# Small SBUF tiles allocated ahead of the large ones in a one-core, two-layer transformer kernel

## The reference, cut to what matters

```python
h = h + nsa_mixer(rmsnorm(h, mix_norm_g), ...)         # w_in 2048 x 5168, compression, w_out 2048 x 2048
z = rmsnorm(h, ffn_norm_g) @ ffn_w_in                  # 2048 x 11264
h = h + (silu(z[..., :D_FF]) * z[..., D_FF:]) @ ffn_w_out   # 5632 x 2048
x = rmsnorm(h, final_norm_g)
proj = _rmsnorm(x, norm_pre_w) @ w_in_2                # 2048 x 16400
... conv + silu, mLSTM over 4 chunks of 64, group pooling ...
merged = sigmoid(g_a) * (y_a @ w_proj_mlstm) + sigmoid(g_b) * (y_b @ w_proj_pool)
return x + _rmsnorm(merged @ w_out_2, norm_post_w)
```

## Time and profile before

| | |
|---|---|
| time, median of 3 runs | 2233.95 us (2227.65 to 2236.28) |
| the profiled execution | 2227.66 us; its span from first to last instruction 2225.6 us |
| TensorE busy (matmuls) | 2175.0 us, 98% |
| weight loads busy | 1894.7 us, 85% |
| VectorE, ScalarE, GpSimd busy | 1453.6 us, 1030.8 us, 176.8 us |
| mean granted TensorE clock | 0.991 |
| chain of work that ended last | 93% TensorE, 4% VectorE |

### The profile page before, as it was taken

How to read it: one execution, slowest core, us unless ns; L and a number is a source line. 1 busy time by engine, 2 the same in 40 slices (tenths; PEclk the granted TensorE clock), 3 DMA queues, 4 the chain that set the end, 5 groups by cost and what they waited for, 6 DMA issues and landing times.

```text
span 2225.6 us, 35012 instructions
## 1 busy us (share of the span) xinstructions
PE 2175.0 (98%) x12502; PEld 1894.7 (85%) x12502; DVE 1453.6 (65%) x1793; ACT 1030.8 (46%) x1342; POOL 176.8 (8%) x215
## 2 busy tenths in 40 slices
PE   8999999999999999999999999999999999999996
PEld 6887889888888888888888888888888888888885
DVE  7746555676666666656666687766867676566575
ACT  4445555354444444443334455444454454444443
POOL 5000222200000000001222000000000000000022
PEclk8999999999999999999999999999999999999998
DMA  6557433365656565655555455555555555555553
GB/s 233 191 189 239 131 107 116 132 200 179 201 181 198 174 204 181 199 186 174 179 182 173 166 180 176 187 168 177 189 163 179 170 188 179 195 189 186 187 181 103
DMA packets 111562, 395.62 MB, mean 178 GB/s; under 512 B 12178, under 2 KB 16290, under 8 KB 111472
## 3 DMA queue, kind: packets, MB, share of 16 engines
q1 hardware_dynamic: 109344, 386.97, 53.4%
q0 software_dynamic: 2128, 7.38, 1.0%
HBM read 389.83 MB, written 2.13 MB: 176 GB/s over the span
## 4 chain that ended last, share of the span: by engine, by line
PE 93%; DVE 4%; issue 1%; ACT 1%; DMA 1%; POOL 0%; ACTq 0%; DVEq 0%; SPq 0%; POOLq 0%
PE set L1367 51%; PE set L1368 26%; PE set L1379 4%; PE set L1380 2%; DVE w_hl L744 1%; DVE x_hl L774 1%; DMA raw<-in_weights 1%; PE set L1357 1%; PE set L1355 1%; PE set L1356 1%; PE misc L1532 1%; PE set L1342 1%; PE set L1344 1%; PE set L1343 1%; PE misc L1518 1%
## 5 line engine op out<-in xcount | busy, mean ns | idle before, releaser
L744 DVE TENSOR_TENSOR w_hl<-raw,w_hl 128x1024 fp32r<-128x1024 f32 x730 | 911.4, 1258 | 573.9 <-ACT w_hl L491 568.6
L1367 PE MATMUL set<-x_hl,w_hl 128*128 128x512 f32 x3584 | 1265.3, 397 | 10.7 <-DVE x_hl L774 9.6
L491 ACT ACTIVATE w_hl<-raw 128x1024 fp32r<-128x1024 f32 x730 | 764.1, 1056 | 856.7 <-PE set L1368 730.5
L1368 PE MATMUL set<-x_hl,w_hl 128*128 128x256 f32 x3584 | 1005.0, 280 | 0.0
L1367 PEld LDWEIGHTS set<-x_hl,w_hl 128*128 128x128 f32 x3584 | 673.9, 188 | 163.8 <-issue 13.3
L1368 PEld LDWEIGHTS set<-x_hl,w_hl 128*128 128x128 f32 x3584 | 679.3, 190 | 0.8
L1367 PE MATMUL set<-f_hl,w_hl 128*128 128x512 f32 x704 | 249.7, 398 | 4.1 <-DVE w_hl L744 4.1
L1368 PE MATMUL set<-f_hl,w_hl 128*128 128x256 f32 x704 | 198.7, 282 | 0.0
L1367 PEld LDWEIGHTS set<-f_hl,w_hl 128*128 128x128 f32 x704 | 133.0, 189 | 37.3 <-DVE w_hl L744 5.1
L498 ACT ACTIVATE cross<-set 128x512 f32<-128x512 f32 (+1 forms) x152 | 88.5, 582 | 138.4 <-PE set L1368 126.9
L1379 PE MATMUL set<-w_hl,x_hl 128*128 128x512 f32 x384 | 134.3, 394 | 4.7 <-DVE w_hl L744 4.7
(11 more groups left out here) (291 smaller groups left out, 2014.3 us busy)
## 6 DMA issues: line engine op xcount, KB each, us to landing
raw<-in_weights SPq DMA_DIRECT2D x730, 512.0 KB, 4.1
bias_g<-bias POOLq DMA_DIRECT2D x4, 572.0 KB, 3.7
cur<-in_cur POOLq DMA_DIRECT2D x4, 535.0 KB, 3.9
h<-in_x SPq DMA_DIRECT2D x4, 512.0 KB, 7.2
bias<-u_dram POOLq DMA_DIRECT2D x1, 2048.0 KB, 13.6
out<-y_t SPq DMA_DIRECT2D x4, 512.0 KB, 3.3
w<-in_w POOLq DMA_DIRECT2D x1, 256.0 KB, 6.8
vm<-in_causal POOLq DMA_DIRECT2D x1, 192.0 KB, 4.3
```

Source lines behind the costliest of these rows:

```text
L491: a(w_hl[at.slot(j)][:, 0, :], raw[at.slot(j)][:, :], ACT.Copy).then_inc(hi_ready, 1)
L744: tt(w_hl[s][:, 1, :], raw[s][:, :], w_hl[s][:, 0, :].bitcast(F32), ALU.subtract).then_inc(lo_ready, 1)
L1367: mm(o, w[:, 0, c], hl[:, kt, :, :], start=first and k == 0, stop=False, skip_group_check=True)
L1368: last = mm(o[:, S:2 * S], w[:, 1, c], hl[:, kt, 0, :], start=False, stop=True, skip_group_check=True)
```

## The change

The tiles `gains`, `gain2`, `rms`, `rtmp`, `ident` and `ones`, and an unused new tile `lead` of 80 bytes, are allocated before `raw` rather than behind `h` and `cross`. In the attention scope `s1c`, `prob` and `bias_g` are allocated before `o_hl`. Nothing else differs: the instructions of every engine, their order and their semaphores are the same, two lines of the file further down.

```diff
+    gains = sb("gains", [P, 5, KT])
+    gain2 = sb("gain2", [P, KT])
+    rms = sb("rms", [P, 5, S + TT])
+    rtmp = sb("rtmp", [P, S + TT])
+    ident = sb("ident", [P, P])
+    ones = sb("ones", [P, P])
+    lead = sb("lead", [P, 20])
     raw = [sb(f"raw{n}", [P, CC]) for n in range(RING)]
     w_hl = [sb(f"w_hl{n}", [P, 2, CC], F32R) for n in range(RING)]
     x_hl = sb("x_hl", [P, KT, 2, S], F32R)
     h = sb("h", [P, KT, S])
-    ident = sb("ident", [P, P])
-    ones = sb("ones", [P, P])
-    gains = sb("gains", [P, 5, KT])
-    gain2 = sb("gain2", [P, KT])
     stat = sb("stat", [P, 2, S])
     sq = sb("sq", [P, FT, S])
     cross = sb("cross", [P, HT, S])
-    rms = sb("rms", [P, 5, S + TT])
-    rtmp = sb("rtmp", [P, S + TT])
...
         with ExitStack() as s1c:
+            prob = [sb(f"prob{n}", [P, PCOLS], scope=s1c) for n in range(2)]
+            bias_g = sb("bias_g", [P, HPG, S + TT * NC], scope=s1c)
             o_hl = sb("o_hl", [P, HEADS, 2, S], F32R, scope=s1c)
-            prob = [sb(f"prob{n}", [P, PCOLS], scope=s1c) for n in range(2)]
             prob_t = sb("prob_t", [P, 2, TRI], scope=s1c)
             prob_ct = sb("prob_ct", [NC, S], scope=s1c)
-            bias_g = sb("bias_g", [P, HPG, S + TT * NC], scope=s1c)
```

## The result

The changed kernel takes 2240.03 us in the median of 16 runs (2235.65 to 2244.96), the kernel before 2234.31 us (2223.19 to 2241.30, 16 runs): a ratio of 1.0032, 95% interval [1.0019, 1.0045]. It is slower, a little, where 0.36% faster was forecast. The stated range, 2214 to 2238, held the old median, not the new one.

What follows compares the result with a forecast made beforehand. TensorE's own instructions were taken to bound the kernel; -3.8 us on `f_hl` and -4.3 on `ya_hl`, `yb_hl`, `m_hl` gave -8.1 from the median 2233.95, forecast 2226 us, range 2214 to 2238.

Steps and rivals of the forecast that it cites:

- TensorE's instructions set the time, and a pair has two rates 6.7 ns apart: Whole kernel: TensorE busy 98% of the span; matmul pairs take 0.3467 us (fast) or about 0.3534 (slow).
- `raw`, `w_hl`, `x_hl`, `h` from 128 to 1728 ... I cost it at nothing.: Weights and `x_hl` move together, keeping their distance, so pairs keep their rhythm: 0 us.
- theory B: Absolute place counts and 1728 is worse than 128; priced as a rival at +22.8 us, 2256.7 us, chance 0.07.
- since most of those steps keep the distance of their operands: Pairs between attention and mLSTM steps: 0 taken, possible -3.8 to +3.8 us from some 570 slow pairs.
- Both signs that the prediction named: Forecast is wrong if `m_hl` keeps 392 to 402 ns, or the up stage lengthens (482.7 us at slow rhythm).
- `ya_hl`, `yb_hl`, `m_hl` ... -4.3 us.: Merge and last projection: 640 pairs at the weights' place turn fast, 6.7 ns each, -4.3 us.
- `f_hl`, -3.8 us.: Down projection: `f_hl` moves to the weights' place, 571 pairs turn fast, 6.7 ns each, -3.8 us.
- one place removes the jump that restores the fast rhythm: Rival: a slow entry into merge would last, its 512 `x_hl` pairs losing 3.4 us; 2233.6 us, chance 0.09.
- At the last pairs before merge the rhythm is fast: Argument, from the kernel before, against the rival that a slow entry into merge would last.
- The range: 2214 to 2238 us, allowing for unknown terms, cases without change and runs 6.3 below and 2.3 above their median.
- The rival of the inherited phase without effect of address: Rhythm is inherited from what precedes, address is not the cause: no change, 2234 us, chance 0.13.
- the bad absolute place: Rival: at 1728 `x_hl` turns slow, about 3400 pairs by 6.7 ns, +22.8 us, 2256.7 us, chance 0.07.

Runs made afterwards that it cites:

- pad_s3: Kernel before with 544 bytes allocated at the start of scope s3, putting `ya_hl`, `yb_hl`, `m_hl` at 128 like `w_hl` and `x_hl`; 2225.09 us, ratio 0.9985.
- a_lead: Changed kernel with `lead` allocated ahead of `ident` and `ones`, moving `ones` from 1120 to 1216 and `ident` with it; 2227.74 us, ratio 0.9994.
- a_again: Changed kernel run once more, nothing altered; 2237.51 us, ratio 1.0038.
- x480: Kernel before with 480 bytes of small tiles between `w_hl` and `x_hl`, so `x_hl` stands 480 bytes behind the weights' place; 2240.70 us, ratio 1.0048.
- a_pad480: Changed kernel with 480 bytes allocated at the start of scope s3, putting `ya_hl`, `yb_hl`, `m_hl` 480 bytes behind the weights' place; 2233.76 us, ratio 1.0020.
- a_step1: Changed kernel with one more single-column matmul in the statistics step ahead of the up stage; 2228.96 us, ratio 1.0019.
- b_again: Kernel before run once more, nothing altered; 2231.15 us, ratio 1.0010.

## Why the prediction was wrong, point by point

- *TensorE's instructions set the time, and a pair has two rates 6.7 ns apart.* Right; it carried the results above, with a third rate at 1600.
- *"`raw`, `w_hl`, `x_hl`, `h` from 128 to 1728 ... I cost it at nothing."* **The step that failed.** The distance between the two did stay, and theory B, the only harm I priced for it, is wrong. But the term took for granted that each pair keeps the rhythm it has, while at distance 0 a stretch takes the rhythm it is entered with. The up stage, 1375 pairs, went from fast by chance (fast in both profiles of before, slow in pad_s3 with the same places) to slow in both profiles, +9.2 us, and no run of 26 has the 2227 us that a fast one would give. The steps between pairs hand the phase on, and they work on small tiles whose distance changed: `ones` stood 512 bytes behind the place of the weights and now stands 608 ahead of it. The prediction took 0 for them as well, "since most of those steps keep the distance of their operands". a_lead shows for merge that such places decide; what makes the up stage's entry slow in every execution is open. Both signs that the prediction named came: `m_hl` kept 90.1 us, with 395 to 403, and the up stage lengthened to 483.0.
- *"`ya_hl`, `yb_hl`, `m_hl` ... -4.3 us."* Measured 0, and +3.4 on `x_hl` between them. The mechanism that I described myself, that a jump in address selects a rhythm, I used for its harm at the border into `ya_hl`; its benefit at the border back I left to a rival. pad_s3 and a_lead have the -4.3 when merge is entered fast.
- *`f_hl`, -3.8 us.* -3.5 in the profile, by luck in part. The stage takes 249.2 to 251.6 us in the eight profiles with `f_hl` at the weights' place, and 250.8 to 254.8 in the eight with it at 1504 or 992 behind: 2.6 us less in the mean, so the place does help. But which stretches are fast differs between executions at either place: in the changed kernel's profile the 200 pairs up to the first wait for VectorE are slow and those behind it fast, and a_again has its second stretch slow as well.
- *The rival "one place removes the jump that restores the fast rhythm".* This is what happened. It had a chance of 0.09 and a price too small: it counted merge, and the longest stretch of the kernel, the up stage, has no jump on its way either. With it the rival comes to 2227.66 + 9.2 + 3.4 - 3.5 = 2236.8, the changed profile's 2236.05. "At the last pairs before merge the rhythm is fast" took the entry of the old kernel for that of the new one.
- *The spread.* The range took the noise of three runs, 6.3 us below the median and 2.3 above. Sixteen runs of the same kernel reach from 2223.19 to 2241.30, and the forecast started from a profile with a fast up stage, which about half of the executions seem to lack.
- *A wrong reference.* For `ident` against `prob` and `prob_t` against `v_g` the prediction names rows 10; they are rows 11.
- *The rival of the inherited phase without effect of address* fell with x480 and a_pad480, though its half on the inherited phase is right; *the bad absolute place* with a_pad480, a_step1 and a_lead.
- *The Trainium skill's rule* (page "TensorE: Matmul & The Clock Gate", Part 2: two independent read ports, so loading weights takes nothing from the running matmul) would have given 0, nearer the result than my sum. But x480 has `x_hl` in merge at 44.9 / 127 = 0.353 us a pair in every round where before and b_again have 0.347, by the place of the operands. The rule does not agree with these traces as it stands, or something else that depends on addresses lies between two matmuls.

## What to carry to other kernels

When the engine that sets the time repeats one instruction at two rates, ask how long each rate lasts and what ends it before counting the slow ones as recoverable; an edit that makes all stretches alike removes what ends the bad rate as well. Read several executions: here both profiles of before showed a fast up stage that comes by chance, and the spread of the runs (2223 to 2241 us) told more than the median. Small tiles and short steps between the long stretches are worth moving, one at a time, once the long ones are known: two such edits of no cost brought the changed kernel from 1.0032 to 0.995 of before.

## What the runs showed of the hardware that was not expected

- Pairs of a 512- and a 256-column matmul, each with its own weight load, run at 0.3467 or 0.3533 us with a granted clock of 1.00 in both (475 to 940 us of the two kernels), for a thousand pairs on end, without a wait. With distance 0 between the stream's and the weights' place the fast form shows 391, or 392 to 395 ns, the slow one 395/398/403.
- The distance of the stream's place from the weights' matters, and of it only what is left over multiples of 512 bytes, as far as tried: 128 against 128, 640 against 640 and 1728 against 1728 are alike, and so are 1504, 992 and 480, slow with 392 to 402. `m_hl` at a distance of 1600 takes 0.3490 us a pair; `x_hl` at 64, which is the same by 512, takes 0.349 in merge and 0.3534 in the up stage.
- A step of a few short matmuls hands the phase of the pairs ahead of it on to those behind it. Ahead of the up stage, in the old order, a slow phase stayed slow in all five profiles that had one. Moving `ident` and `ones` by 96 bytes was enough to turn 1152 pairs. Why is not settled: no run shows what the two reads share.
